# Splitting weight blocks of a two-layer decoder: a ring of four, GpSimd for the high half, VectorE for the low half

## What is computed

```python
# every layer: pre-RMSNorm token mixer -> pre-RMSNorm cross-attention (4 heads) into
#   256 memory tokens -> pre-RMSNorm SwiGLU FFN, each with a plain residual add.
D_MODEL = 1024; SEQ = 512; DEPTH = 2; N_MEM = 256
D_FF = 2816        # gate and up: 1024 x 5632, down: 2816 x 1024
out = rms_norm(trunk(x, mem))
```

## Time and profile before

| what | value |
|---|---|
| median of 3 runs | 1483.05 us (1481.87 to 1483.18) |
| span of the profiled execution, first to last instruction | 1481.1 us |
| PE busy | 1394.9 us (94%) |
| DVE busy | 753.8 us (51%) |
| POOL busy | 872.5 us (59%) |
| ACT busy | 343.8 us (23%) |
| mean granted TensorE clock | 0.969 |

### The profile page before, as it was taken

The page is one execution under the profiler, slowest core; times in us unless marked ns, Lnnn a source line. Parts: engine busy times, 40 slices in busy tenths (PEclk is TensorE's granted clock), DMA queues, the critical chain, the costliest instruction groups (busy, mean ns, idle before and its releaser), DMA issues.

```text
span 1481.1 us, 17229 instructions
## 1 busy us (share of the span) xinstructions
PE 1394.9 (94%) x6296; PEld 1131.8 (76%) x6296; DVE 753.8 (51%) x875; ACT 343.8 (23%) x718; POOL 872.5 (59%) x576
## 2 busy tenths in 40 slices
PE   5999956999999999999999988999999999999997
PEld 4888745578777888888888777877777888888886
DVE  5876999504748344004333888827564442023332
ACT  4326204511233111001111214632331110001122
POOL 4666645446555666666666655346565666666662
PEclk9999987999999999999999997999999999999998
DMA  5232321013222332233323321013222332333221
GB/s 194 81 114 85 100 64 57 16 57 124 85 73 75 100 96 91 97 100 100 99 93 93 105 94 44 1 43 100 71 71 86 93 94 97 100 100 98 91 96 57
DMA packets 90239, 127.14 MB, mean 86 GB/s; under 512 B 5440, under 2 KB 53824, under 8 KB 90176
## 3 DMA queue, kind: packets, MB, share of 16 engines
q1 hardware_dynamic: 90176, 126.27, 26.9%
HBM read 124.15 MB, written 2.10 MB: 85 GB/s over the span
## 4 chain that ended last, share of the span: by engine, by line
PE 78%; DVE 17%; issue 3%; ACT 1%; DMA 0%; SPq 0%; DVEq 0%; ACTq 0%
PE ps L494 22%; PE ps L497 22%; PE ps L498 22%; PE ps L622 4%; PE ps L589 4%; DVE acc L845 3%; PE ps L605 2%; DVE rope L892 2%; DVE rope L891 1%; DVE h L863 1%; DVE z_lo L839 1%; DVE xc L1097 1%; DVE lru_d L1087 1%; DVE xc L1095 1%; DVE rope L890 1%
## 5 line engine op out<-in xcount | busy, mean ns | idle before, releaser
L443 POOL TENSOR_TENSOR w_lo<-raw,w_hi 128x1024 fp32r<-128x1024 f32 x222 | 555.9, 2504 | 18.5
L441 POOL TENSOR_SCALAR w_hi<-raw 128x1024 fp32r<-128x1024 f32 x222 | 250.4, 1128 | 489.9 <-issue 350.5
L494 PE MATMUL ps<-z_hi,w_hi 128*128 128x512 f32 x1072 | 426.5, 398 | 6.2 <-DVEq L885 3.0
L497 PE MATMUL ps<-z_lo,w_hi 128*128 128x512 f32 x1072 | 421.3, 393 | 0.0
L498 PE MATMUL ps<-z_hi,w_lo 128*128 128x512 f32 x1072 | 421.1, 393 | 0.0
L494 PEld LDWEIGHTS ps<-z_hi,w_hi 128*128 128x128 f32 x1072 | 204.2, 190 | 52.3 <-issue 5.0
L497 PEld LDWEIGHTS ps<-z_lo,w_hi 128*128 128x128 f32 x1072 | 204.3, 191 | 44.9 <-issue 2.7
L494 PE MATMUL ps<-f_hi,w_hi 128*128 128x512 f32 x608 | 238.2, 392 | 0.2 <-DVEq L1004 0.2
L498 PE MATMUL ps<-f_hi,w_lo 128*128 128x512 f32 x608 | 236.7, 389 | 0.0
L498 PEld LDWEIGHTS ps<-z_hi,w_lo 128*128 128x128 f32 x1072 | 203.7, 190 | 43.1
L497 PE MATMUL ps<-f_lo,w_hi 128*128 128x512 f32 x608 | 236.6, 389 | 0.0
(11 more groups left out here) (162 smaller groups left out, 1263.1 us busy)
## 6 DMA issues: line engine op xcount, KB each, us to landing
raw<-in_w_gate_up SPq DMA_DIRECT2D x176, 256.0 KB
raw<-in_w_down SPq DMA_DIRECT2D x44, 512.0 KB
raw<-in_w_in SPq DMA_DIRECT2D x28, 512.0 KB
raw<-in_w_out SPq DMA_DIRECT2D x20, 512.0 KB
raw<-in_xa_wkv SPq DMA_DIRECT2D x16, 512.0 KB
raw<-in_xa_wq SPq DMA_DIRECT2D x8, 512.0 KB
raw<-in_xa_wo SPq DMA_DIRECT2D x8, 512.0 KB
raw<-in_w_qkv SPq DMA_DIRECT2D x8, 512.0 KB
```

The source lines that it names most:

```text
L441: pool.tensor_scalar(w_hi[:, half], raw[:, j], 1.0, 1.0, ALU.mult, ALU.mult).then_inc(s_hi, 1)
L443: pool.tensor_tensor(w_lo[:, half], raw[:, j], w_hi[:, half].bitcast(F32), ALU.subtract).then_inc(s_split, 1)
L494: ins = pe.matmul(o, whi, rhi, start=start, stop=False)
L497: pe.matmul(o, whi, rlo, start=False, stop=False)
```

## The change

The two rings (four `raw`, two `w_hi`, two `w_lo`) become one of four slots: four `raw` and four `w_hi` buffers, and `w_lo` lies over `raw` in the same memory, so that the subtraction writes in place. The bytes are the same. A slot is free for its next load only when PE is through with its unit: SP waits for `s_used` of unit u-3 in place of the split of unit u-4. POOL rounds only, and waits for the load only. The subtraction of all 226 units goes to DVE, at places written out by hand in its list (`low_to(k)`: do all units below k that are not done yet). The subtractions sit in the norm loops, in the attention loops, in the first layer's list and four to each feed-forward group. The two units of each cross-attention that DVE split wholly now go the same way as all. POOL's list in an attention has two units behind `normalise` of head 0, one behind that of head 1, and one behind that of head 4 (or 3). The load of mask0 goes ahead of the fourth unit of `attn0`.

```diff
-RAW = 4
-SPLIT = 2
+SLOTS = 4
+FIRST_TURN = {0: 1, 1: 2, 3: 3, 5: 4, 7: 6}
+def split_turns(second, end):
+    return {-1: second + 3, 0: min(second + 4, end + 2), 1: min(second + 5, end + 2), 2: min(second + 6, end + 2),
+            3: end + 2, 5: end + 3, 7: end + 4, DB: end + 6}
...
-        w_hi = at("w_hi", [P, SPLIT, 2, 512], F32R, z_wh)
-        w_lo = at("w_lo", [P, SPLIT, 2, 512], F32R, z_wl)
+        w_hi = at("w_hi", [P, SLOTS, 2, 512], F32R, z_wh)
+        w_lo = at("w_lo", [P, SLOTS, 2, 512], F32R, z_raw)
...
@@ SP: unit
-                if u_static >= RAW:
-                    sp.wait_ge(s_split, u - RAW + 1)
+                if u_static >= SLOTS:
+                    sp.wait_ge(s_used, u - SLOTS + 2)
...
@@ POOL
-                pool.tensor_scalar(w_hi[:, half], raw[:, j], 1.0, 1.0, ALU.mult, ALU.mult).then_inc(s_hi, 1)
-                pool.wait_ge(s_hi, u + 1)
-                pool.tensor_tensor(w_lo[:, half], raw[:, j], w_hi[:, half].bitcast(F32),
-                                   ALU.subtract).then_inc(s_split, 1)
...
+            def high_part(u, slot):
+                pool.wait_ge(s_raw[slot], (u - slot + SLOTS) * (32 // SLOTS))
+                pool.sem_inc(s_begun, 1)
+                pool.tensor_scalar(w_hi[:, slot], raw[:, slot], 1.0, 1.0, ALU.mult, ALU.mult).then_inc(s_hi, 1)
...
+                high(at_unit, first + 4)
                 for n in range(ATTN[name]["heads"]):
                     normalise(ATTN[name], n)
                     if n == 0:
+                        high(first + 4, first + 6)
+                    if n == 1:
+                        high(first + 6, first + 7)
+                    if n == min(4, ATTN[name]["heads"] - 1):
+                        high(first + 7, first + 8)
...
@@ PE, at each unit
-                    pe.wait_ge(s_split, u0 + j + 1)
+                    pe.wait_ge(s_lo, u0 + j + 1)
...
@@ DVE
+            def low_part(u, u_static):
+                slot = u_static % SLOTS
+                dve.wait_ge(s_hi, u + 1)
+                dve.tensor_tensor(w_lo[:, slot], raw[:, slot], w_hi[:, slot].bitcast(F32), ALU.subtract).then_inc(s_lo, 1)
...
@@ DVE: residual
+                if done:
+                    low_to(turn[-1])
                 for m in range(DB if done else 0):
                     dve.wait_ge(done, m + 1)
...
+                    low_to(turn.get(m, 0))
                 if norm_next:
                     for m in range(DB - lag if done else 0, DB):
                         low(m)
+                        if not done:
+                            low_to(FIRST_TURN.get(m, 0))
+                if done:
+                    low_to(turn[DB])
...
@@ DVE: attention, loop over n
                     if n < H:
                         maxima(n)
+                    if n == 0:
+                        low_to(u0 + 4)
...
                     if n == 1:
-                        for i in range(a["dve_splits"]):
-                            split(UNIT0[a["name"]] + 2 + i)
+                        low_to(u0 + 5)
                         if n in extra:
                             extra[n]()
+                        low_to(u0 + 6)
                         for b in range(2):
                             dve.wait_ge(a["s_filler"], b + 1)
...
+                    if n == 2:
+                        low_to(u0 + 7)
                     if 2 <= n < H + 2 and a["turned_first"]:
                         turned(n - 2)
...
+                    if n == 5:
+                        low_to(u0 + 8)
...
@@ DVE: first layer
+                    low_to(UNIT0["in_xy"] + 2 * m0_ + 6 + min(i + 1, 4))
...
+                    if m0_ == 0:
+                        low_to(UNIT0["in_xy"] + 10 + m + 1)
+            low_to(UNIT0["gates"] + LRU_HEADS)
...
                 dve.tensor_tensor(xc[:, m, :], gate_i[:, m % 2, :], xc[:, m, :], ALU.mult).then_inc(s_gx, 1)
+                if m % 2:
+                    low_to(UNIT0["in_qkv"] + m // 2 + 1)
...
                 decay(m)
+                if m % 2:
+                    low_to(UNIT0["in_qkv"] + 4 + m // 2 + 1)
...
                 qk_tile(t)
+                low_to(UNIT0["in_qkv"] + 8 + t + 1)
...
                 qk_tile(t)
+                low_to(UNIT0["attn0"] + t - 4 + 1 if t < 7 else 0)
...
@@ DVE: layer 1
                         qkv1(q1[:, t, :], s_done["qkv_q0"], "qkv_q0", t, t)
+                        low_to(q1_unit + 2 + t // 2 + 1)
                     for t in range(4):
                         rotate_q(t)
+                        low_to(q1_unit + 4 + t // 2 + 1)
+                    low_to(q1_unit + 7)
                     for t in range(4, 8):
                         qkv1(q1[:, t, :], s_done["qkv_q1"], "qkv_q1", t - 4, t)
+                    low_to(q1_unit + 8)
                     memory_low(1)
+                    low_to(q1_unit + 9)
...
                     rotate_q(5)
+                    low_to(UNIT0["attn1"] + 4)
...
@@ DVE: feed-forward group, up0 + 6 + r + 4 s + 8 i
                             dve.tensor_tensor(ff_g[:, p, :], ps[:, b0 + p, :], rstd[:], ALU.mult).then_inc(s_ff_gate, 1)
+                        low_next(0)
...
                         dve.nop().then_inc(s_free[g_static % 2], 4)
+                        low_next(1)
...
                         dve.wait_ge(s_ff_lo, 2 * n + 2)
+                        low_next(2)
+                        low_next(3)
```

More of the change, by code:

```diff
@@ L408, in _ @@
                     sp.dma_start(m1[:], mask1).then_inc(s_mask1, 16)
-                stream(f"attn{l}", xa_wkv[l], 4, count=1)
                 if l == 0:
-                    sp.wait_ge(s_done["in_qkv"], 12)
-                    sp.dma_start(m0[:], mask0).then_inc(s_mask0, 16)
+                    for j in range(4):
+                        if j == 3:
+                            sp.wait_ge(s_done["in_qkv"], 12)
+                            sp.dma_start(m0[:], mask0).then_inc(s_mask0, 16)
+                        unit(UNIT0["attn0"] + j, [(0, 512, rows(xa_wkv[0], 2 * P * j, 0))])
+                else:
+                    stream("attn1", xa_wkv[1], 4, count=1)
                 stream(f"out{l}", (w_out0, w_out1)[l], (6, 4)[l])
@@ L465, in normalise, with high, body @@
                 ins.then_inc(a["s_prob"], 1)
-            split(0, 0, empty=True)
-            split(1, 1, empty=True)
-            at_unit = SPLIT
+            def high_part(u, slot):
+                pool.wait_ge(s_raw[slot], (u - slot + SLOTS) * (32 // SLOTS))
+                pool.sem_inc(s_begun, 1)
+                pool.tensor_scalar(w_hi[:, slot], raw[:, slot], 1.0, 1.0, ALU.mult, ALU.mult).then_inc(s_hi, 1)
+            def high(u0, u1):
+                while u0 % SLOTS and u0 < u1:
+                    high_part(u0, u0 % SLOTS)
+                    u0 += 1
+                def body(i):
+                    for j in range(SLOTS):
+                        high_part(i * SLOTS + (u0 + j), j)
+                loop(pool, (u1 - u0) // SLOTS, body)
+                for u in range(u0 + (u1 - u0) // SLOTS * SLOTS, u1):
+                    high_part(u, u % SLOTS)
+            at_unit = 0
             for name in ("attn0", "xattn0", "attn1", "xattn1"):
-                last = UNIT0[name] + 4
-                split_all(at_unit, last - ATTN[name]["dve_splits"])
+                first = UNIT0[name]
+                high(at_unit, first + 4)
                 for n in range(ATTN[name]["heads"]):
@@ L832, in _, with low_to, residual @@
             link = chain.link
-            def residual(norm, done, bias=None, group0=0, norm_next=True):
+            told = [0]
+            def low_part(u, u_static):
+                slot = u_static % SLOTS
+                dve.wait_ge(s_hi, u + 1)
+                dve.tensor_tensor(w_lo[:, slot], raw[:, slot], w_hi[:, slot].bitcast(F32), ALU.subtract).then_inc(s_lo, 1)
+            def low_to(u1):
+                for u in range(told[0], min(u1, UNITS)):
+                    low_part(u, u)
+                told[0] = max(told[0], min(u1, UNITS))
+            def residual(norm, done, bias=None, group0=0, norm_next=True, units=()):
+                turn = split_turns(*units) if done else {}
                 def low(m):
@@ L1132, in _ @@
             attention(ATTN["attn0"], {0: lambda: late_recurrence(4), 1: lambda: late_recurrence(6)})
-            residual("xa0", s_done["out0"], group0=GROUP0["out0"])
+            residual("xa0", s_done["out0"], group0=GROUP0["out0"], units=(UNIT0["out0"] + 6, UNIT0["xq0"]))
             for l in (0, 1):
@@ L1173, in _ @@
                     attention(ATTN["attn1"], {1: lambda: [rotate_q(6), rotate_q(7)]})
-                    residual("xa1", s_done["out1"], bias="b_out", group0=GROUP0["out1"])
+                    residual("xa1", s_done["out1"], bias="b_out", group0=GROUP0["out1"],
+                             units=(UNIT0["out1"] + 4, UNIT0["xq1"]))
                 one_over_rms(f"xa{l}")
@@ L1179, in _ @@
                 attention(ATTN[f"xattn{l}"])
```

(10 more changed lines are left out.)

65 lines of the change are left out of this document (20 added, 45 removed).

## The result

The changed kernel takes 1486.82 us (median of 5 runs, 1485.60 to 1489.25) where the kernel before, on the same chip, takes 1481.87 (1480.98 to 1483.18): a ratio of 1.0037, 95% interval 1.0024 to 1.0049. It is slower, by 5 us or 0.4%, which is small but clear of the interval. The prediction had 10 us. The profiled execution has a span of 1487.5 us against 1481.1: it was the slowest of its five, so the two traces differ by 6.4 us.

What follows compares the result with a forecast made beforehand. It took PE, busy 94% of the span, as the bound, with changes possible only where PE stands still. Its terms, -4.6 - 3.8 - 6.3 + 2.6 + 8.4 + 3 + 10.8, gave +10.1 us: 1493.2 us, range 1470 to 1504.

Steps and rivals of the forecast that it cites:

- Item 1 and 2: Start and DVE's first-layer list: less stretching outweighs new subtractions and waits for roundings, -4.6 us together.
- Item 3: Norms of xa0 and xa1: `acc` complete before PE wants it, so the stalls go, -3.8 and -6.3 us.
- mix1: Norm in layer 1: would give 2.2 us, used up by the later waits of layer 1.
- Item 4: Two norms behind `xo`: `acc` at 466.4 to 466.8 against 465.5 before, +1.3 us each, +2.6.
- the stall stays: Norms behind `xo`: PE still stands before the sum until `acc` is complete, +1.3 us each.
- Item 5: Two cross-attentions: PE starts the values 4.2 us late, +8.4 for two, and +3 for the lower clock.
- Item 6: Layer 1: DVE waits for roundings before and in the attention, +9.6 us and +1.2 at n = 5.
- 3 us idle: Layer 1's attention, n = 2: DVE waits 3 us for `normalise`(1) and another rounding.
- +1.2 at n = 5: Layer 1's attention: further loss at n = 5, 1.2 us, beside 9.6 up to the values of head 0.
- Rival A: Attentions: waits hidden because scores and exponentials are late; faster, 1471 us; chance 0.25.
- Rival B: Attentions cost half (-11) and the rest holds, so gains and losses cancel: 1482 to 1483 us; chance 0.18.
- Rival C: Residual loops: subtractions hold up every one, `acc` late at xa0 and xa1 too; much slower, 1503 us; chance 0.15.

Runs made afterwards that it cites:

- e7: e4 with eight first-layer subtractions of `in_qkv` (units 3 to 10) one place later and the last behind `recur(1)`: 1456.23 us, 0.9830.
- e9: Changed kernel with the subtraction back on POOL, behind its rounding, in the ring of four; DVE has none: 1480.68 us, 1.0000.
- e5: e4 with the subtraction of `up` 1 moved from behind h(0) to behind h(3) in both loops behind `xo`: 1454.81 us, 0.9817.
- e1: Changed kernel with the subtraction of n = 2 moved behind `turned(0)` in DVE's list, in all four attentions: 1475.84 us, 0.9967.
- e4: e1 with the n = 1 subtractions moved too: each attention's four stand at the ends of n = 2, 3, 4 and 5: 1462.37 us, 0.9871.
- e8: e4 with later subtractions in the first layer, in layer 1 and in the loops behind `xo`, all together: 1443.35 us, 0.9745.

## Why the prediction was right in its sign and too high in its size

The forecast was 1493.2, the result 1486.8: on the side forecast and inside the wide range of 1470 to 1504, a hair below the forecast's own 1487 to 1499. The loss was half of the one forecast. Its sum was +10.1; the spans differ by 6.4. One item is off by -8.3 us, and the others, off by +1.3, -0.4, +1.5 and +2.3, hide more than half of that. By its own items:

- **Item 1 and 2** (start and first layer): -4.6 forecast, -3.3 measured. DVE's waits for roundings were where the walk had them, 9.6 us together for about 8, but the one in front of `memory_low` was 4.9 us and not 2. e7 shows that these places held back 5 to 6 us.
- **Item 3** (norms of xa0, xa1): -3.8 and -6.3 forecast, -4.0 and -6.5 measured. The size came straight from the windows and was right. The cause given, stretching gone, is enough for it but not needed: e9 gets nearly the same with the stretching still there, by `acc` coming 1.6 and 3.2 us nearer to PE's arrival. In the changed kernel `acc` had 4.6 us to spare at xa0 and 1.2 at xa1, more than the 2.5 and 0.4 of the walk. mix1 gave 2.4, for 2.2.
- **Item 4** (norms behind `xo`): +2.6 forecast, -5.7 measured. **This is the term that failed, by 8.3 us, more than the whole error.** Its time for `acc` was good: complete at 465.27 in the changed kernel, in a stage that starts 0.72 earlier, thus at 466.0 on the old scale, against 466.4 to 466.8 forecast. What failed is "the stall stays", that is, setting the lateness of `acc` against PE's old time of arrival. PE arrives later by itself. The wait of 4.43 us in front of h(1), which the item had counted for `acc`, also delays h(3) and so PE's first unit of `up` by 1.86 us; with the first unit of `up` partly at the lower clock (7.2 us for 5.44) PE reaches the sum at 465.1, when `acc` is nearly there. One stall of 3.54 us with a stretch at 1.2 GHz behind it has become one of 1.86 with a shorter such stretch: over `up`'s first three units and the last of `xo` 5.2 us are lost, 7.3 before. e5 confirms that one wait in DVE's list made both ends late: without it both go.
- **Item 5** (cross-attentions): 4.2 + 1.5 us each forecast, +6.5 and +6.4 measured; the wait was 4.09. The mechanism is shown by e1 and e4. The lower clock cost 2.4 us each, near the 2.5 named as its bound, not the middle that was taken.
- **Item 6** (layer 1): +10.8 net of mix1 forecast, +13.1 measured. Up to the values of head 0 the walk was good: they come 10.1 us later against the start of `qkv_q0`, for 9.6, and the wait before them is the place named:

```profile
914.62 1.23 DVE L839 TENSOR_TENSOR w_lo<-raw,w_hi 128x1024 fp32r<-128x1024 f32 x1 [2.88 <-POOL w_hi L454]
915.77 0.55 DVE L985 COPY prob_t<-ps 128x384 f32<-128x384 f32 x1
```

```profile
916.37 0.90 PE L621 MATMUL ps<-prob_t,v 128*64 128x128 f32 x3 [13.37 <-DVE prob_t L985]
```

"3 us idle" at n = 2 was 2.88. What was too small is the second term, "+1.2 at n = 5". PE is 9.9 us late at head 3, and heads 4 and 5 add 1.7 and 1.6 us, 3.2 in all. There the subtraction waits again for a rounding that stands behind a `normalise`, and PE for the copy behind it; its clock is at a mean of 0.72 in the 4 us that follow:

```profile
933.28 1.23 DVE L839 TENSOR_TENSOR w_lo<-raw,w_hi 128x1024 fp32r<-128x1024 f32 x1 [1.84 <-POOL w_hi L454]
...
937.74 2.25 PE L621 MATMUL ps<-prob_t,v 128*64 128x128 f32 x14 [1.59 <-DVE prob_t L985]
```

None of the moves touches this place, and e8 still loses 3.3 us there.

**The step that failed**, then, is item 4's "the stall stays: +1.3 each": it set `acc` against an arrival of PE that the same wait had moved, and the runs show -5.7 us in its place. With this item alone put right the sum would have been +1.8, too low, since items 1, 2, 5 and 6 were all taken too lightly. That the total came as near as it did is in part luck.

Rival A (the attention waits are hidden) is refuted for this order of work, but what it priced is real: with those waits taken out, e4 is at 1462, below even its 1471. Rival B (the attentions cost half) is refuted too: items 5 and 6 cost 26.0 us where 22.2 were forecast. Rival C did not happen: `acc` was in time at xa0 and xa1, and in the loops behind `xo`, which did wait for a rounding, PE was late as well.

The Trainium skill's rule (SBUF — State Buffer, Who interferes with whom) has an exclusive lock that a VectorE instruction with two SBUF inputs and a GpSimd instruction that reads SBUF take in turn, whole. The traces agree: the additions above end 0.54 to 0.55 us after POOL's instruction, be it of 1.16 or 2.11 us, and so do the 18 additions of the kernel before that began during a subtraction of POOL (median 2.71 us for the subtraction, 2.88 for the addition). And `h<-ps,h`, which has one input in SBUF, takes 0.688 us on the mean in e8 and 0.692 in e9, with POOL 22% or 60% busy. The 3 us that its rule would have added to the forecast for POOL's own delay did not show: the roundings in front of the waits at n = 2 took 1.04 us (cross-attention 0) and 1.05 us (layer 1).

## What to carry to other kernels

Moving work off an engine that stretches its neighbour's instructions was worth 39 us here and first measured as a loss. That happens when the moved instruction has to wait for another engine and is written where its data become ready instead of where they are wanted. Put an instruction that waits behind everything in its list that PE needs sooner, and count a wait only if it is the last one ahead of that. When a consumer's input becomes later, walk through what else the same wait makes late, the consumer's own arrival first.

## What was not expected of the hardware

- The stretching of a DVE instruction depends on the POOL instruction it meets and not on POOL's busy share: an addition of 0.68 us became 1.53, 2.38 or 2.88 by a POOL instruction of 1.16, 2.11 or 2.71 us. A POOL form that takes 0.84 us more (1.894 against 1.054 us, medians) for the same values cost the kernel 40 to 43 us.
- Waits of 2.78 and 2.77 us of PE in the same code left the clock at 2.4 GHz once and at 1.2 GHz once. What happens behind a wait of this length can't be priced from its length alone.
- Which DVE instructions POOL's hit is a matter of phase. The ring alone left POOL's subtraction at 2.49 us on the mean (2.50 before) and the total unchanged, yet it took 3 to 6 us from each of the norms of xa0 and xa1 and added 2.5 and 3.3 us behind `xo`.
